# Scaled rows of the last four groups: by GpSimd and a transpose, in place of a product with a diagonal

## What is computed

```python
def rms_norm_2(x, g):
    xf = x.astype(jnp.float32)
    y = xf * lax.rsqrt(jnp.mean(xf * xf, axis=-1, keepdims=True) + EPS)
    return (y * g.astype(jnp.float32)).astype(x.dtype)

# second block, start (seam 2 below): x is the output of the first block
h = rms_norm_2(x, g_pre_mix[l]) * (1.0 + sc1) + sh1
z = h @ w_in[l]
...
# second block, feed-forward (seam 4 below)
x = x + gt1 * rms_norm_2(mix, g_post_mix[l])
h = rms_norm_2(x, g_pre_ffn[l]) * (1.0 + sc2) + sh2
u = causal_dwconv(h @ w_up[l], conv_w[l], conv_b[l])
```

## Time and profile before

| | us |
|---|---|
| runs | 1907.67, 1907.77, 1908.87 |
| the profiled execution, its own time | 1907.67 |
| its span | 1905.9 |
| TensorE busy in the span | 1887.9 (99%) |
| VectorE busy | 1365.9 (72%) |
| ScalarE busy | 1038.6 (54%) |
| GpSimd busy | 102.5 (5%) |

### The profile page before, as it was taken

How to read it: one execution, slowest core, us unless ns; L and a number is a source line. 1 busy time by engine, 2 the same in 40 slices (tenths; PEclk the granted TensorE clock), 3 DMA queues, 4 the chain that set the end, 5 groups by cost and what they waited for, 6 DMA issues and landing times.

```text
span 1905.9 us, 30030 instructions
## 1 busy us (share of the span) xinstructions
PE 1887.9 (99%) x9891; PEld 1601.8 (84%) x9891; DVE 1365.9 (72%) x1889; ACT 1038.6 (54%) x1689; POOL 102.5 (5%) x168
## 2 busy tenths in 40 slices
PE   9999999999999999999999999999999999999998
PEld 7888888888889988888888788888888888888886
DVE  7777776677767666678777877777777766655555
ACT  6545546654545444457654445666656666544444
POOL 3000001000010102211100000000000000000000
PEclk9999999999999999999999999999999999999999
DMA  9887786697777864476678885777777766465653
GB/s 309 290 304 261 243 279 215 213 314 275 273 277 263 274 192 133 134 225 201 215 256 282 298 297 167 232 237 236 231 232 244 233 200 190 157 205 191 197 194 137
DMA packets 233225, 443.52 MB, mean 233 GB/s; under 512 B 14363, under 2 KB 108197, under 8 KB 232000
## 3 DMA queue, kind: packets, MB, share of 16 engines
q1 hardware_dynamic: 229840, 428.27, 68.0%
q0 software_dynamic: 3248, 14.29, 2.6%
q10 hardware_dynamic: 64, 0.02, 0.0%
HBM read 438.28 MB, written 4.24 MB: 232 GB/s over the span
## 4 chain that ended last, share of the span: by engine, by line
PE 94%; DVE 2%; DMA 2%; ACT 1%; issue 1%; ACTq 0%; SPq 0%; DVEq 0%
PE PS L2039 55%; PE PS L2529 17%; PE PS L2533 9%; PE PS L2409 2%; DMA ada_raw<-in_w_ada 1%; PE PS L2419 1%; PE PS L2198 1%; PE PS L2207 1%; PE PS L2094 1%; PE PS L2217 1%; PE PS L2218 1%; PE PS L2103 1%; DVE w_lo L1252 1%; PE PS L2215 1%; ACT w_hi L702 1%
## 5 line engine op out<-in xcount | busy, mean ns | idle before, releaser
L2039 PE MATMUL PS<-w_hi,aT 128*128 128x512 f32 (+1 forms) x3264 | 1045.2, 394 | 2.1 <-DVE arena L1731 1.1
L1252 DVE TENSOR_TENSOR w_lo<-raw,w_hi 128x1024 fp32r<-128x1024 f32 (+2 forms) x624 | 755.5, 1215 | 397.8 <-ACT w_hi L702 390.2
L702 ACT ACTIVATE w_hi<-raw 128x1024 fp32r<-128x1024 f32 (+2 forms) x624 | 651.3, 1047 | 568.8 <-PE PS L2039 324.6
L2039 PEld LDWEIGHTS PS<-w_hi,aT 128*128 128x128 f32 x3264 | 611.7, 188 | 132.9 <-issue 4.8
L2039 PE MATMUL PS<-w_lo,aT 128*128 128x512 f32 (+1 forms) x1632 | 633.0, 388 | 0.0
L2529 PE MATMUL PS<-aT,w_hi 128*128 128x512 f32 x1408 | 442.9, 396 | 1.1 <-DVE aT L1421 1.1
L2039 PEld LDWEIGHTS PS<-w_lo,aT 128*128 128x128 f32 x1632 | 307.0, 188 | 58.9 <-issue 0.2
L2533 PEld LDWEIGHTS PS<-aT,w_lo 128*128 128x128 f32 x1408 | 264.5, 188 | 62.5
L2533 PE MATMUL PS<-aT,w_lo 128*128 128x256 f32 x1408 | 276.6, 278 | 0.0
L1310 DVE SCALAR_TENSOR_TENSOR arena<-ada_raw,silu_c,arena 128x1024 f32<-128x1024 f32 x192 | 246.1, 1282 | 29.5 <-DMA ada_raw<-in_w_ada 29.4
L2529 PEld LDWEIGHTS PS<-aT,w_hi 128*128 128x128 f32 x1408 | 214.4, 189 | 1.8 <-issue 1.8
(11 more groups left out here) (271 smaller groups left out, 1392.7 us busy)
## 6 DMA issues: line engine op xcount, KB each, us to landing
raw<-in_w_in SPq DMA_DIRECT2D x248, 512.0 KB, 4.2
ada_raw<-in_w_ada SPq DMA_DIRECT2D x192, 512.0 KB, 4.8
raw<-in_w_up SPq DMA_DIRECT2D x176, 512.0 KB, 3.6
raw<-in_w_down SPq DMA_DIRECT2D x88, 512.0 KB, 4.3
raw<-in_w_out SPq DMA_DIRECT2D x32, 512.0 KB, 5.0
raw<-in_w_o SPq DMA_DIRECT2D x32, 512.0 KB, 5.6
raw<-in_w_uq SPq DMA_DIRECT2D x24, 384.0 KB, 3.8
raw<-in_w_ukv SPq DMA_DIRECT2D x16, 512.0 KB, 6.0
```

The lines of the kernel that those rows point to most:

```text
L702: nc.scalar.activation(part_of(w_hi, m, width), part_of(raw, m, width), ACT.Copy).then_inc(hi_ready, 1)
L1252: nc.vector.tensor_tensor(part_of(w_lo, m, width), part_of(raw, m, width), part_of(w_hi, m, width).bitcast(F32), ALU.subtract).then_inc(lo ...
L2039: mm = pe.matmul(dst, l, r, start=first and j == 0, stop=last and j == 2)
```

## The change

A new tile view, `LATE` (the two halves of `qkT`), holds one group of scaled rows, 128 x 256 for each row tile. At both seams POOL runs through the last four groups: for each row tile it waits, then multiplies the 256 columns of X by the row's inverse root into `LATE` and counts up `late_rows`. For the first late group it waits for `rows_ready` (the same event that says the diagonal is there); for the next ones for `rows_T`, which says that PE has turned the group before, since there is only one buffer. PE waits for `late_rows` and turns the group with four transposes by the identity. Groups 0 to 3 stay as they were. POOL's DMAs at L617 and L688 come behind the four groups.

```diff
+        LATE = qkT[:, :].rearrange("p (s n) -> p s n", s=ST)
+        late_rows = sem("late_rows")
@@ block.gpsimd @@
+            def scale_late(j, at, turned, x2=False):
+                for s in range(ST):
+                    if j == SKEW:
+                        pool.wait_ge(rows_ready, turned[1] + s)
+                    else:
+                        pool.wait_ge(rows_T, turned[0] + j - SKEW)
+                    if x2:
+                        pool.wait_ge(x2_ready, 4 * s + j // 2 + 1)
+                    nc.gpsimd.tensor_scalar(LATE[:, s, :], X[:, s, SEQ * j:SEQ * (j + 1)], stat[:, 8 + at + s:9 + at + s],
+                                            None, ALU.mult).then_inc(late_rows, 1)
@@ seam 2 @@
+            for j in range(SKEW, SLOTS):
+                scale_late(j, 6, (T_SEAM_2 + 2 * SKEW, 3))
             pool.wait_ge(rows_ready, 4)
             for s in range(ST):
                 nc.gpsimd.dma_start(x1_dram[s * P:(s + 1) * P, :], X[:, s, :]).then_inc(x_saved, 16)
@@ seam 4 @@
             nc.gpsimd.dma_start(ADA_GT2[0:1, :], b_ada_2[:, GT2 * D:(GT2 + 1) * D]).then_inc(ffn_row_landed, 16)
+            for j in range(SKEW, SLOTS):
+                scale_late(j, 2, (T_SEAM_4 + SKEW, 7), x2=True)
             pool.wait_ge(rows_ready, 8)
             nc.gpsimd.dma_start(G_FFN, bass.AP(g_post_ffn_2.tensor, 0, [[0, P], [1, D]])).then_inc(ffn_row_landed, 16)
@@ block.tensor @@
+            def late_group(j, n, banks):
+                pe.wait_ge(late_rows, n)
+                for k in range(2):
+                    for s in range(ST):
+                        tr = pe.transpose(PS[:, banks + j % 4, SEQ * k + P * s:SEQ * k + P * (s + 1)],
+                                          LATE[:, s, P * k:P * (k + 1)], ident[:])
+                tr.then_inc(rows_T, 1)
@@ seam 2 @@
                     if s == 1:
                         mm.then_inc(chunk_used, 1)
-                        unit_T(2 * SKEW + slot, B_T)
+                        late_group(SKEW + slot, 2 * slot + 2, B_T)
@@ seam 4 @@
                 if slot < SKEW:
                     pe.wait_ge(x2_ready, 7 + slot // 2)
-                    for s in range(ST):
-                        mm = scaled_rows(SKEW + slot, s, B_UP1)
-                    mm.then_inc(rows_T, 1)
+                    late_group(SKEW + slot, SLOTS + 2 * slot + 2, B_UP1)
```

## The result

The changed kernel takes 1914.25 us (median of six runs, 1913.7 to 1917.12) against 1907.94 for the kernel before in the same session: a ratio of 1.0037, 95% interval 1.0027 to 1.0047. It is slower by 6.3 us; the forecast was 1907.6, with 1904.4 to 1910.8 around it.

What follows compares the result with a forecast made beforehand. The prediction took TensorE, busy 1887.9 of 1905.9 us, as the bound. Seam 2 at +1.5 us and seam 4 at -1.5 summed to 0.0 against the profiled 1907.67 us; it gave 1907.6, range 1904.4 to 1910.8.

Steps and rivals of the forecast that it cites:

- a group is 0.45 us cheaper: Late groups at both seams: plain transposes reach the next product in 0.36 us instead of 0.81, saving 3.6 us in all.
- The price of a scaling: POOL's 16 scalings at both seams: 0.40 us each, bounds 0.40 and 0.73, from a copy and a two-tensor product.
- One turn at the port for each scaling: Both seams: a scaling meeting a two-SBUF-input DVE instruction ends about 0.26 us after it and costs DVE 0.14 us.
- the lock that the forecast cites: Aside on the port pair DVE and POOL share: exclusive for a whole instruction, costing DVE 0.26 us more per scaling.
- Seam 2 ahead of the late groups: Group 4's two scalings at each diagonal delay DVE 0.14 us each, 0.3 us in all; bounds 0 and 2 x 0.40.
- The walk of seam 2: Waits before groups 5, 6, 7 of 1.66, 0.6, 0.7 us, together 3.0; seam 2 in all +1.5 us.
- Seam 4, -1.5 us: Seam 4 in all: 1.8 us gained, 0.2 lost before the first late group, 0.1 at row tile 0's residuals.
- I take no wait: Last three late groups of seam 4: 2.47 us of room, about 1.9 to 2.5 needed; at most 0.5 wait each.
- What is moved: X-saving DMAs start about 14 us later, the gain row lands with 6 us to spare; no cost in time.
- the second, POOL too slow: Rival: scalings take 0.73 us or meet long DVE instructions, seam 2 most; 1909.6 to 1911.1 us, chance 0.17.
- the break-even: Both seams break even where a pair of scalings at seam 2 takes 2.06 us from start to end.
- The third, the clock: Rival: TensorE's clock falls to 1.2 GHz in the new waits for about 7 us; +3.5, 1911.1 us, chance 0.08.

Runs made afterwards that it cites:

- e4_copy: The changed kernel with all its waits, but POOL copies the rows instead of multiplying by the inverse root: 1908.46 us against 1908.35 for the kernel before, ratio 0.9999.
- e8_two_tensors: Against a kernel with four late-group buffers (1904.91 us), POOL multiplies two tensors instead of using a column factor: 1905.97 us, ratio 0.9989 to the kernel before.
- e2_seam_2_only: The change at seam 2 alone, with seam 4 as in the kernel before: 1917.05 us, ratio 1.0041 to the kernel before.
- e6_kept_busy: The changed kernel plus 30, 4 and 12 unused TensorE transposes ahead of groups 5, 6 and 7 at seam 2: 1918.22 us, ratio 1.0046 to the kernel before.
- e7_constant: The changed kernel with all its waits, but POOL multiplies by the constant 0.5 instead of a column factor: 1911.32 us, ratio 1.0014 to the kernel before.

## Why the prediction was wrong, point by point

- TensorE is the bound, a group is 0.45 us cheaper, 3.6 us in all: right. 0.36 us to the next product in the trace, 4.6 (with 3.6 in the interval) in the run that has nothing else.
- The price of a scaling: this is the step that failed. The text took 0.40 with 0.73 as the upper bound, "nearer to the copy" because it has one input tensor. Measured: 0.93 alone. The two nearest rows were not two ends of a scale with the unknown instruction between them; an instruction that multiplies by one factor lay above the one with two tensors. The estimate worked out from the Trainium skill (GPSIMD Engine Reference, "Elementwise — side-by-side cycle accounting"), 0.38 us, seemed to confirm the lower end, and was as far off: even with a constant it is 0.85.
- One turn at the port for each scaling, and 0.14 us for DVE: the turns were read from copies, and for copies they are right (`e4_copy`). With a factor from a column it is two turns, 2.49 against 1.39 us. DVE loses about 0.2 us at a time (the cast of 515.42 takes 0.62 in place of 0.42), and 0.4 beside the products of `e8_two_tensors`. By the lock that the forecast cites from the Trainium skill (SBUF — State Buffer, "SBUF: two separate sides") it would be the whole POOL instruction, up to 0.93 us here; the measured loss decides, and the 0.14 of the rows was nearer to it, if too low.
- Seam 2 ahead of the late groups, +0.3 us: right. From the first group to the first late group it is 512.51 - 498.48 = 14.03 us, before 511.41 - 497.60 = 13.81.
- The walk of seam 2, +1.5 us: by its own steps right (`e4_copy`), its durations wrong. 3.0 us of waits were 7.5, of which at most 0.8 us are the clock's.
- Seam 4, -1.5 us: +1.4 in the trace, and no difference that can be told in the run with seam 4 alone. "I take no wait" for three pairs rested on the same 0.40; they took 2.94 to 3.34 us where 2.47 was the room, and the groups came 0.6, 0.6 and 1.0 us late, beyond the "at most 0.5". The first late group came 1.0 us late, not 0.2: its scaling behind the residual took 2.01 us.
- What is moved costs nothing: no row speaks against it. At 1179.64 the gain row's DMA starts and lands 8.0 us later, ahead of the end of the split at 1190.02 + 1.23 = 1191.25: 3.6 us to spare, not 6. The view of waits has no wait that follows from it.
- The rivals: the second, POOL too slow, was the true one, with the break-even named (2.06 us for a pair; the pairs took 5.40, 1.90 and 2.72), at a chance of 0.17 and a price of at most +3.5, since its worst scaling was 0.73 us. The third, the clock, came with it and not in its place, for half of its 7 us and mostly hidden under the waits. Counted apart, neither reached 1914; the text did not add them, though the one sets the length of the idle time that the other depends on.
- The range: its upper end was made from bounds that were no bounds.

## What to carry to other kernels

An engine that is nearly idle isn't free when its result goes round in a loop with the bound engine: price one turn of the loop (here transposes, two scalings, back) against the room that the bound engine leaves, and if the trace has no row of that very instruction and operand form, measure it alone and beside the neighbour that shares its port before trusting it. When the turn is too long, buffers that let the slow engine run ahead can be worth more than a faster instruction. Here four in place of one turned +6 us into -3 us with the same scaling.

## What the runs showed of the hardware that had not been expected

- On POOL, 128x256 float32: by a factor from a column 0.926 us, by a constant 0.850, two tensors 0.724, a copy 0.404.
- Beside a stream of DVE subtractions of two SBUF tensors the column factor costs 2.49 us, the constant 1.36; beside the DVE form that has a column factor itself, 1.44; beside copies of one SBUF input, 1.41; beside one with an input in PSUM, 0.926.
- DVE's own loss is smaller than POOL's: subtractions of 1.22 us take 1.41 beside the constant, and 1.63 beside a product of two tensors on POOL (`e8_two_tensors`).
- TensorE's granted clock stayed at 1.00 through an idle time of 4.2 us at seam 2 and fell to 0.50 (1.2 GHz) when the work had begun again, for 3.4 us. The length of the idle time alone doesn't say whether it falls: behind 1.97 us in `e2_seam_2_only` and 2.56 in `e6_kept_busy` it fell, behind 2.04 in `e7_constant` it did not.
